# Last stage of an encoder step: gate product on GpSimd, residual added by TensorE in PSUM, two VectorE operations a tile

## What is computed

```python
y = moe_0 * wts_0 + moe_1 * wts_1              # grouped_experts
x = x + g2[:, None, :] * y                     # g2: the gate from adaLN
y_out = x * rsqrt(mean(x * x) + EPS) * norm_f  # final RMSNorm
```

## Time and profile before

| | |
|---|---|
| median of 3 runs | 2189.5 us (2187.33 to 2193.02) |
| the profiled execution, its own time | 2199.07 us |
| its span, first to last instruction | 2197.4 us |
| mean granted TensorE clock | 0.966 of 2.4 GHz |
| last stage, `first(0)` to the end of `finish(8)` | 2146.76 to 2194.35 us |

### The profile page before, as it was taken

One profiled execution on the slowest core, in us unless ns is written; L12 is line 12 of the kernel. 1 busy time (PEld: TensorE's weight loads), 2 busy tenths in 40 slices (PEclk: granted clock), 3 DMA queues, 4 the chain that ended last, 5 costly groups with the idle time before them and its releaser, 6 DMA issues. The chain is left out here.

```text
span 2197.4 us, 30354 instructions
## 1 busy us (share of the span) xinstructions
PE 2017.9 (92%) x11833; PEld 1729.7 (79%) x11833; DVE 1339.2 (61%) x1793; ACT 1069.1 (49%) x1401; POOL 341.6 (16%) x271
## 2 busy tenths in 40 slices
PE   5998999999987999999999999997899999999970
PEld 2887777777755799999999999786788888888860
DVE  3523565555564255566354444476799888888858
ACT  3422443443343255564343333222677887777744
POOL 1000000000001212221001001232123322222100
PEclk8999999999998999999999999998899999999985
DMA  7313111113378311125454487335799999999956
GB/s 252 105 61 100 60 60 58 48 59 114 100 247 282 89 41 30 41 66 166 136 164 140 137 239 184 121 112 203 278 376 365 380 381 388 390 378 388 380 196 258
DMA packets 247541, 415.95 MB, mean 189 GB/s; under 512 B 23688, under 2 KB 187272, under 8 KB 221811
## 3 DMA queue, kind: packets, MB, share of 16 engines
q1 hardware_dynamic: 234546, 383.43, 50.8%
q0 software_dynamic: 10944, 24.01, 2.9%
q10 hardware_dynamic: 1920, 6.70, 0.8%
HBM read 382.65 MB, written 45.66 MB: 195 GB/s over the span
## 5 line engine op out<-in xcount | busy, mean ns | idle before, releaser
L397 DVE TENSOR_TENSOR ew_lo<-region,ew_hi 128x2048 fp32r<-128x2048 f32 x192 | 431.7, 2286 | 35.7 <-ACT ew_hi L2183 35.3
L2183 ACT ACTIVATE ew_hi<-region 128x2048 fp32r<-128x2048 f32 x192 | 367.9, 1918 | 120.0 <-DMA region<-in_w 118.7
L397 DVE TENSOR_TENSOR wm_lo<-weights,wm_hi 128x1024 fp32r<-128x1024 f32 x91 | 124.6, 1372 | 144.1 <-ACT wm_hi L1312 143.2
L2667 PE MATMUL PS<-ew_lo,xT_hi 128*128 128x512 f32 x512 | 203.5, 397 | 9.8 <-issue 9.4
L2669 PE MATMUL PS<-ew_hi,xT_hi 128*128 128x512 f32 x512 | 201.0, 393 | 0.0
L2668 PE MATMUL PS<-ew_hi,xT_lo 128*128 128x512 f32 x512 | 200.6, 392 | 0.0
L1467 DVE CUSTOM_DVE_ANT_0 region<-PS,region 128x896 f32<-128x896 f32 (+7 forms) x128 | 91.9, 755 | 146.0 <-PE PS L1718 146.0
L1312 ACT ACTIVATE wm_hi<-weights 128x1024 fp32r<-128x1024 f32 x92 | 97.1, 1057 | 130.8 <-DMA weights<-in_w_pa 70.5
L1190 ACT ACTIVATE region<-region,small 128x896 f32<-128x896 f32 (+7 forms) x128 | 98.8, 772 | 119.0 <-DVE small L1467 119.0
L404 PE MATMUL PS<-h_lo,wx_hi 128*128 128x384 f32 x384 | 133.5, 348 | 3.2 <-POOL wx_lo L397 3.2
L405 PE MATMUL PS<-h_hi,wx_lo 128*128 128x384 f32 x384 | 129.2, 337 | 0.0
(11 more groups left out here) (421 smaller groups left out, 4778.6 us busy)
## 6 DMA issues: line engine op xcount, KB each, us to landing
region<-in_w SPq DMA_DIRECT2D x192, 1024.0 KB, 7.8
weights<-in_w_gate SPq DMA_DIRECT2D x46, 512.0 KB, 4.0
region<-in_w_mod SPq DMA_DIRECT2D x20, 1024.0 KB, 5.5
weights<-in_w_in SPq DMA_DIRECT2D x36, 512.0 KB, 4.0
weights<-in_w_pb SPq DMA_DIRECT2D x24, 512.0 KB, 3.6
weights<-in_w_pa SPq DMA_DIRECT2D x24, 512.0 KB, 3.7
region<-F_d SPq DMA_DIRECT2D x16, 512.0 KB, 6.1
weights<-in_cache_k SPq DMA_DIRECT2D x8, 1024.0 KB, 8.2
```

Of the source, the lines that this page charges most:

```text
L397: return eng.tensor_tensor(lo, x, hi.bitcast(F32), ALU.subtract)
L2183: act(ewh[u], ew[u], ACT.Copy).then_inc(sem(f"eu_hi{u}"), 1)
L2667: mm(out, lh(c), ewl[u][:, c, :], start=first and c == 0, stop=False)
```

## The change

Each tile's work is spread over four engines:

- `first(t)` (ScalarE) writes `y0 * w0` to PSUM banks 6 and 7 (`first_ps`), one buffer; it waits until `combine(t-1)` has read it. It waits for y0 alone, since the two loads now have a semaphore each.
- `combine(t)` (VectorE) is one operation, `acc = y1 * w1 + first_ps`, with semaphore `both`.
- GpSimd multiplies `acc` by `G2` in place, semaphore `c_g`.
- TensorE adds: `residual(t)` multiplies x by the identity into `x2_ps[t % 3]` (banks 0-1, 2-3 or 4-5), two fp32 matmuls of 128x512; `update(t)` accumulates `acc` by the identity on top, two more, semaphore `x2_mm`.
- `squares` and `finish` read `x2_ps[t % 3]` in PSUM.
- Orders: VectorE `combine(t+2)`, `finish(t)`. ScalarE `squares(t)`, `root(t)`, `first(t+3)`. TensorE `residual(0)`, `residual(1)`, `residual(2)`, then `update(t)`, `residual(t+3)`, where `residual(t+3)` waits for `finish(t)`.

```diff
@@ buffers
+        x2_ps, first_ps = [banks(2 * j, 2) for j in range(3)], banks(6, 2)
@@ SyncE
-                        e.dma_start(y01[k][t], y2_d[...]).then_inc(sem(f"y_in{t}"), 16)
+                        e.dma_start(y01[k][t], y2_d[...]).then_inc(sem(f"y{k}_in{t}"), 16)
@@ GpSimd
+                e.wait_ge(sem("g2_in"), MOD_LOAD + 16)
+                for t in range(NT):
+                    e.wait_ge(sem("both"), t + 1)
+                    e.tensor_tensor(acc[t % RING], acc[t % RING], G2[t == PT_], ALU.mult).then_inc(sem("c_g"), 1)
@@ ScalarE, first
-                    if t >= RING:
-                        e.wait_ge(sem("o_made"), t - RING + 1)
-                    e.wait_ge(sem(f"y_in{t}"), 32)
-                    act(acc[j], y01[0][t], ACT.Copy, scale=wts[:, 0, t:t + 1]).then_inc(sem("y0w"), 1)
+                    if t:
+                        e.wait_ge(sem("both"), t)
+                    e.wait_ge(sem(f"y0_in{t}"), 16)
+                    act(first_ps, y01[0][t], ACT.Copy, scale=wts[:, 0, t:t + 1]).then_inc(sem("y0w"), 1)
@@ ScalarE, squares
-                    e.wait_ge(sem("x2_made"), t + 1)
+                    e.wait_ge(sem("x2_mm"), t + 1)
...
-                    act(out_t[j], acc[j], ACT.Square, accum_out=ssq3[:, j:j + 1]).then_inc(sem("ss3"), 1)
+                    act(out_t[j], x2_ps[t % 3], ACT.Square, accum_out=ssq3[:, j:j + 1]).then_inc(sem("ss3"), 1)
@@ ScalarE, order
                 first(0)
+                first(1)
+                first(2)
                 for t in range(NT):
-                    if t + 1 < NT:
-                        first(t + 1)
                     squares(t)
                     root(t)
+                    if t + 3 < NT:
+                        first(t + 3)
@@ VectorE
-                    st.did(stt(out=acc[j], in0=y01[1][t], scalar=wts[:, 1, t:t + 1], in1=acc[j], op0=ALU.mult, op1=ALU.add))
-                    st.wait()
-                    st.did(tt(acc[j], acc[j], G2[t == PT_], ALU.mult))
-                    st.wait()
-                    tt(acc[j], acc[j], x1b[:, t, :], ALU.add).then_inc(sem("x2_made"), 1)
+                    if t >= RING:
+                        e.wait_ge(sem("x2_mm"), t - RING + 1)
+                    stt(out=acc[j], in0=y01[1][t], scalar=wts[:, 1, t:t + 1], in1=first_ps, op0=ALU.mult, op1=ALU.add).then_inc(sem("both"), 1)
...
-                    stt(out=out_t[j], in0=acc[j], scalar=rst3[:, j:j + 1], in1=NF, op0=ALU.mult, op1=ALU.mult).then_inc(sem("o_made"), 1)
+                    stt(out=out_t[j], in0=x2_ps[t % 3], scalar=rst3[:, j:j + 1], in1=NF, op0=ALU.mult, op1=ALU.mult).then_inc(sem("o_made"), 1)
@@ TensorE
+                def residual(t):
+                    if t >= 3:
+                        e.wait_ge(sem("o_made"), t - 2)
+                    for k in range(2):
+                        mm(x2_ps[t % 3][:, 512 * k:512 * (k + 1)], ident[:], x1b[:, t, 512 * k:512 * (k + 1)], start=True, stop=False)
+
+                def update(t):
+                    e.wait_ge(sem("c_g"), t + 1)
+                    for k in range(2):
+                        last = mm(x2_ps[t % 3][:, 512 * k:512 * (k + 1)], ident[:], acc[t % RING][:, 512 * k:512 * (k + 1)], start=False, stop=True)
+                    last.then_inc(sem("x2_mm"), 1)
+                residual(0)
+                residual(1)
+                e.wait_ge(sem("yo_A"), more * 2 + 2 * NE)
+                residual(2)
+                for t in range(NT):
+                    update(t)
+                    if t + 3 < NT:
+                        residual(t + 3)
```

More of the change, by code:

```diff
@@ L2045, in _ @@
                     for k in range(2):
-                        e.dma_start(y01[k][t], y2_d[k * TOK + t * P:k * TOK + (t + 1) * P, :]).then_inc(sem(f"y_in{t}"), 16)
+                        e.dma_start(y01[k][t], y2_d[k * TOK + t * P:k * TOK + (t + 1) * P, :]).then_inc(sem(f"y{k}_in{t}"), 16)
                 for t in range(NT):
@@ L2250, in first @@
                 def first(t):
-                    j = t % RING
-                    if t >= RING:
-                        e.wait_ge(sem("o_made"), t - RING + 1)
-                    e.wait_ge(sem(f"y_in{t}"), 32)
-                    act(acc[j], y01[0][t], ACT.Copy, scale=wts[:, 0, t:t + 1]).then_inc(sem("y0w"), 1)
+                    if t:
+                        e.wait_ge(sem("both"), t)
+                    e.wait_ge(sem(f"y0_in{t}"), 16)
+                    act(first_ps, y01[0][t], ACT.Copy, scale=wts[:, 0, t:t + 1]).then_inc(sem("y0w"), 1)
                 def squares(t):
                     j = t % RING
-                    e.wait_ge(sem("x2_made"), t + 1)
+                    e.wait_ge(sem("x2_mm"), t + 1)
                     if t >= RING:
                         e.wait_ge(sem(f"o_out{j}"), 16 * (t // RING))
-                    act(out_t[j], acc[j], ACT.Square, accum_out=ssq3[:, j:j + 1]).then_inc(sem("ss3"), 1)
+                    act(out_t[j], x2_ps[t % 3], ACT.Square, accum_out=ssq3[:, j:j + 1]).then_inc(sem("ss3"), 1)
                 def root(t):
@@ L2534, in combine @@
                     j = t % RING
-                    e.wait_ge(sem(f"y_in{t}"), 32)
+                    e.wait_ge(sem(f"y1_in{t}"), 16)
                     e.wait_ge(sem("y0w"), t + 1)
-                    st.did(stt(out=acc[j], in0=y01[1][t], scalar=wts[:, 1, t:t + 1], in1=acc[j], op0=ALU.mult, op1=ALU.add))
-                    st.wait()
-                    st.did(tt(acc[j], acc[j], G2[t == PT_], ALU.mult))
-                    st.wait()
-                    tt(acc[j], acc[j], x1b[:, t, :], ALU.add).then_inc(sem("x2_made"), 1)
+                    if t >= RING:
+                        e.wait_ge(sem("x2_mm"), t - RING + 1)
+                    stt(out=acc[j], in0=y01[1][t], scalar=wts[:, 1, t:t + 1], in1=first_ps, op0=ALU.mult, op1=ALU.add).then_inc(sem("both"), 1)
                 def finish(t):
@@ L2547, in finish @@
                     st.wait()
-                    stt(out=out_t[j], in0=acc[j], scalar=rst3[:, j:j + 1], in1=NF, op0=ALU.mult, op1=ALU.mult).then_inc(sem("o_made"), 1)
+                    stt(out=out_t[j], in0=x2_ps[t % 3], scalar=rst3[:, j:j + 1], in1=NF, op0=ALU.mult, op1=ALU.mult).then_inc(sem("o_made"), 1)
+                combine(0)
+                combine(1)
                 for t in range(NT):
[L2550 to L2553, removed]
+                    if t + 2 < NT:
+                        combine(t + 2)
+                    finish(t)
             @block.tensor
```

## The result

The changed kernel takes 2212.65 us in the median of 7 runs, the one before 2193.02 in 7 runs taken with them: a ratio of 1.0076, 95% interval 1.006 to 1.0093, or +16.7 us (13 to 20; the two medians themselves lie 19.6 us apart). It is slower. The prediction had the sign and the chain of waits, with +6.7 us and a range of 2187 to 2203 for the time; the measured time lies outside.

What follows compares the result with a forecast made beforehand. Bound: a serial loop through four engines at mostly 1.2 GHz. finish(8) ends at 2157.05 + 6 x 6.93 - 0.8 + 3.2 = 2201.0 against 2194.35, +6.7 us; on the 2189.5 median, 2196.2, range 2187 to 2203.

Steps and rivals of the forecast that it cites:

- the sign: Whole kernel: slower, by +6.7 us or +0.31%; slower by over 0.3% had chance 0.48.
- the chain of waits: Last stage: update(t+1) stands behind residual(t+3), which waits for finish(t); tiles run in series, 6.93 us each at 1.2 GHz.
- residual + update together cost 3.69 or 1.99 us: TensorE's four fp32 matmuls a tile, last stage: 3.69 us at 1.2 GHz or 1.99 at 2.4 GHz.
- the remark that the rows show two passes: TensorE's fp32 matmuls: about 0.43 us for 512 columns at 2.4 GHz, taken as two passes instead of four.
- the third rival: TensorE's matmuls take four passes, twice the row's time: loop 10.3 us, about +33 us, 2222; chance 0.03.
- the rest of the chain: Each loop outside TensorE's part: 0.15 to TensorE, 0.10 to ScalarE, 2.99 from Square to the last operation.
- the start: Stage up to the end of finish(0): 2157.05 or so against 2156.97 before, about +0.1 us.
- the tail: Last two tiles, updates 7 and 8 following update 6 at once: 1.5 to 1.7 us each, 3.2 for both.
- The clock: TensorE in the last stage's loop: mostly 1.2 GHz, with 0.8 us given back for blocks catching the upper level.
- Rival 2: GpSimd's product at 4.08 us or VectorE stalled beside it at 3.19: total 2198 to 2202 us; chance 0.07.
- Rival 4: Three banks let the last stage's tiles overlap, pitch 2.8 to 3.7 us: -9 us, 2180; chance 0.03.
- The first rival: TensorE is granted 2.4 GHz in the loop, 5.23 us a turn: -3.2 us, 2186.3; chance 0.12.

Runs made afterwards that it cites:

- e1: Changed kernel with only TensorE's order altered: residual(t+2) placed behind update(t), so it waits for finish(t-1); 2185.97 us, ratio 0.9957 to the kernel before.
- e3: Changed kernel with order and all waits kept, but residual(3) to residual(8) issue no matmul; 2207.92 us, ratio 1.0049 to the kernel before.
- e5: Changed kernel plus three zero-weight fp32 matmuls behind each update(t) up to t = 5, keeping TensorE busy; 2204.58 us, ratio 1.004 to the kernel before.
- e4: Changed kernel keeping only GpSimd's product: TensorE does nothing, VectorE adds x itself, everything but first in SBUF; 2203.04 us, ratio 1.003 to the kernel before.
- e7: Changed kernel with e1's order, fp32r update, Square's output over y0, and Sqrt table loaded early; 2178.53 us, ratio 0.9917 to the kernel before.

## Why the prediction was wrong

*The chain.* Right. `residual(t+3)` waits for `finish(t)`, `update(t+1)` stands behind it, and six tiles run one after another; the waits show it, and e1, which changes only that order, takes it away and 26 us with it.

*The step that failed: "residual + update together cost 3.69 or 1.99 us".* They cost 3.70 us at 2.4 GHz, and in the longest turn, where the clock rose on the way (0.56), 6.6. I took the 16 records of line 738 and the 8 of line 1718 for as many calls, so "four successive 512-column steps" were in truth two. The loop in the code, two times four calls, would have said so beside the x16. With it goes the remark that the rows show two passes: a call is 2 x 0.43 = 0.86 us, about four times the 0.23 us from one to the next of the experts' fp32r records of the same 128x512 at 2.4 GHz (2135.75 to 2135.98 in the kernel before), so the rule of four passes in the Trainium skill ("FP8 and Floating Point Precision", section "TensorE Precision Notes") agrees with this trace, and the third rival, which had 0.03, was right about the matmul. It was wrong about the total (+33), because it kept the lower clock: its turn of 10.3 us would have been wholly at 1.2 GHz, and none was.

In the sum: TensorE's part of the six turns was 46.6 - 6 x 3.05 = 28.3 us instead of 6 x 3.69 - 0.8 = 21.3, so +7.0; the rest of the chain gave back 1.1, the start added 2.3 and the tail 0.2. That is 8.3 us, the difference between +15.0 and the forecast's +6.7.

*The clock.* Forecast: mostly 1.2 GHz. Measured 0.84 in the loop: three of six turns wholly at 2.4 GHz, three mixed. In those three the matmuls began after a wait of 3.05 us and still had the upper level, so the remark that such bursts start at the lower level each time does not hold here. The two errors have one root and act against each other: with twice the work, TensorE is busy 3.7 of 6.75 us and keeps the upper level longer than I thought. e3 halves its work, and the turn becomes 6.83 us at 1.2 GHz, which is what the prediction had (6.93) for the work that it had counted. That the turns of 6.75 us lie inside the forecast's 6.5 to 7, and their 3.70 us of TensorE on its 3.69, is luck: twice the work at twice the clock. The rest of the chain, 0.15 + 0.10 + 2.99 = 3.24, was nearly right: e3's turn less its 3.78 us of TensorE is 3.05, and so is 6.75 less 3.70.

*The start.* Forecast +0.1, measured +2.4. Most of it is the same doubling: six calls of `residual` are twelve records, 6.83 us from the first to `update(0)` where 5.2 was forecast. The rest is that TensorE left its empty loop 4.8 us after the loads' issue and not 3.7, in this execution (3.9 in e1's); why is not shown. So `residual` ends at 2151.8, not before the product; the product itself came when forecast, 0.16 us after `combine(0)` ended plus its 2.35. GpSimd's 4.08 did not occur (2.34 to 2.36 each).

*The tail, VectorE, ScalarE, GpSimd.* The last two tiles took 1.72 us each, forecast 1.5 to 1.7; that too is luck, since the 1.7 stood for two matmuls at 1.2 GHz and these were two at 2.4 of twice the price. VectorE's 1.28, Square's 1.02 and GpSimd's 2.35 were as forecast, with no stall on VectorE. Rival 2 fell. Rival 4, tiles that overlap, is what e1 does; it needed another order, as said.

*The first rival* was half right: 2.4 GHz for most of the loop, but with 5.23 us a turn only if the matmuls had cost half.

What stays open: the 1.7 us between the stage's +15.0 and the measured +16.7 are within the interval and were not looked for. Nor do the runs say why three of the six turns kept the upper clock to the end and three did not; e5 shows only what that costs.

## What to carry to other kernels

A ring of three buffers overlaps nothing if the instruction that waits for a buffer stands in the queue ahead of work that is ready: put the refill of a buffer one step further back in the queue, behind the next piece of ready work, so that the `finish` it waits for is the one of a tile earlier. When an operation is priced by rows of another line, count that line's calls in the code beside its records. On TensorE less work can cost as much time as more, when the rest is waiting and the clock falls: here half the matmuls took as long a turn (e3).

## Not expected of the hardware

A turn of the loop took 6.75 us with eight records of fp32 matmul (granted clock 1.00 from 2166 to 2172.8) and 6.83 with four (3.78 us of TensorE, e3). Adding 2.6 us of useless matmuls to each turn (e5) made the kernel 8 us faster. A VectorE operation of 1.28 us with two SBUF operands takes 2.95 beside a GpSimd product (e4), and 1.28 if one operand is in PSUM (e1). The first store, issued while the eighteen loads of 512 KB were still landing, landed 9.5 to 12.5 us after its issue (changed kernel 9.5, e1 10.8, e7 12.5), and once the loads had landed a store took 2.6 us; so the slot of the first store came free late.
